# The last gate tile of a decode step cut in halves around two transposes, and six value loads issued from ScalarE

## What is computed

```python
h = rmsnorm(x, norm_attn)
qa, ka, va, qb, kb, vb, qc, gate_logits = split(h @ w_in)      # gate_logits: 3 x 1024 per token
# decode: 8 sequences, caches of 128 (a), 2048 read at strides 1, 4, 16 (b), 256 (c) rows
oa = gathered_attention(qa, [cache_swa_k; ka], [cache_swa_v; va], idx_a, sink)
ob = dilated_sample(qb, [cache_dil_k; kb], [cache_dil_v; vb], 2048)
oc = memory_attention(qc, cache_mem_k, cache_mem_v)
g = sigmoid(gate_logits).reshape(B, L, 3, 1024)
merged = g[:, :, 0] * (oa @ w_br_a) + g[:, :, 1] * (ob @ w_br_b) + g[:, :, 2] * (oc @ w_br_c)
x = x + merged @ w_out
x = x + moe_ffn(rmsnorm(x, norm_ffn), ...)                     # top 4 of 32 experts, 12.6 MB of weights each
```

## Time and profile before

| | us |
|---|---|
| median of 3 runs | 1260.06 (1259.14 to 1262.4) |
| the profiled execution, its own time | 1257.38 |
| its span in the profile | 1255.5 |
| PE busy | 1202.7 (96%) |
| DVE busy | 410.5 (33%) |
| ACT busy | 233.7 (19%) |
| mean DMA rate over the span | 400 GB/s |

### The profile page before, as it was taken

One profiled execution on the slowest core, in us unless ns is written; L12 is line 12 of the kernel. 1 busy time (PEld: TensorE's weight loads), 2 busy tenths in 40 slices (PEclk: granted clock), 3 DMA queues, 4 the chain that ended last, 5 costly groups with the idle time before them and its releaser, 6 DMA issues.

```text
span 1255.5 us, 14690 instructions
## 1 busy us (share of the span) xinstructions
PE 1202.7 (96%) x6122; PEld 516.6 (41%) x6122; DVE 410.5 (33%) x917; ACT 233.7 (19%) x459; POOL 74.2 (6%) x79
## 2 busy tenths in 40 slices
PE   9999999999999999999998999899999999899996
PEld 4456678775533333333333333333333333333332
DVE  3275653335531422314132222313131323222233
ACT  2212433230210210111211011111011121101112
POOL 0453000510200000000000000000000000000000
PEclk9999999999999999999999999999999999999998
DMA  9999999999999999999999999999999999999994
GB/s 337 388 312 365 325 352 355 269 346 395 353 409 429 428 434 433 431 434 429 429 433 431 433 432 432 431 430 432 432 432 431 430 431 432 433 433 421 430 425 172
DMA packets 64712, 502.36 MB, mean 400 GB/s; under 512 B 5872, under 2 KB 30064, under 8 KB 48112
## 3 DMA queue, kind: packets, MB, share of 16 engines
q1 hardware_dynamic: 62784, 497.10, 97.1%
q0 software_dynamic: 848, 2.36, 0.6%
q10 hardware_dynamic: 1008, 1.90, 0.4%
HBM read 498.42 MB, written 37.03 MB: 426 GB/s over the span
## 4 chain that ended last, share of the span: by engine, by line
PE 58%; DMA 33%; SPq 5%; DVE 2%; issue 1%; ACT 0%; DVEq 0%; ACTq 0%
PE ps L1902 19%; DMA ring<-in_w_gate_up 19%; PE ps L1945 11%; DMA high<-in_w_gate_up 6%; PE ps L1268 6%; DMA high<-in_w_down 4%; PE ps L1799 3%; DMA low<-in_w_gate_up 3%; PE ps L1354 3%; PE ps L1861 3%; PE ps L1649 2%; SPq L610 2%; PE ps L1662 2%; DMA ring<-in_w_in 2%; PE ps L1818 1%; PE ps L1330 1%
## 5 line engine op out<-in xcount | busy, mean ns | idle before, releaser
L1902 PE MATMUL ps<-ring,high 128*64 128x512 f32 x1216 | 272.3, 595 | 17.8 <-DMA ring<-in_w_gate_up 17.6
L1902 PEld LDWEIGHTS ps<-ring,high 128*64 128x64 f32 x1216 | 85.8, 136 | 181.7 <-issue 155.1
L1945 PE MATMUL ps<-ring,high 128*64 128x512 f32 x608 | 138.2, 596 | 0.7 <-issue 0.7
L1354 PE MATMUL ps<-low,ring 128*128 128x288 f32 x384 | 102.1, 413 | 0.3 <-DMA ring<-in_w_in 0.3
L1150 ACT ACTIVATE high<-ps 128x512 f32<-128x512 f32 x32 | 19.1, 597 | 439.8 <-PE ps L1921 439.8
L1902 PE MATMUL ps<-high 128*64 128x512 f32 x416 | 93.4, 595 | 7.8 <-DMA high<-in_w_gate_up 7.8
L1902 PE MATMUL ps<-low,high 128*64 128x512 f32 x416 | 93.0, 595 | 5.2 <-DMA low<-in_w_gate_up 5.2
L2443 DVE TENSOR_REDUCE low<-ps 128x1 f32<-128x288 f32 x15 | 6.9, 458 | 274.5 <-PE ps L1831 274.5
L1354 PEld LDWEIGHTS ps<-low,ring 128*128 128x128 f32 x384 | 69.7, 190 | 22.5 <-issue 5.3
L1945 PEld LDWEIGHTS ps<-ring,high 128*64 128x64 f32 x608 | 42.6, 136 | 75.4 <-issue 72.2
L2471 DVE TENSOR_TENSOR x_tok<-x_tok,ps 64x512 f32<-64x512 f32 (+2 forms) x48 | 41.3, 860 | 74.7 <-PE ps L1861 72.4
(11 more groups left out here) (381 smaller groups left out, 1198.8 us busy)
## 6 DMA issues: line engine op xcount, KB each, us to landing
ring<-in_w_gate_up SPq DMA_DIRECT2D x28, 4096.0 KB, 38.1
ring<-in_w_down SPq DMA_DIRECT2D x14, 4096.0 KB, 40.6
ring<-in_w_gate_up SPq DMA_DIRECT2D x20, 2048.0 KB, 26.9
high<-in_w_gate_up SPq DMA_DIRECT2D x10, 4096.0 KB, 37.7
low<-in_w_gate_up SPq DMA_DIRECT2D x9, 4096.0 KB, 38.4
ring<-in_w_down SPq DMA_DIRECT2D x10, 2048.0 KB, 19.4
low<-in_w_down SPq DMA_DIRECT2D x5, 4096.0 KB, 38.9
high<-in_w_down SPq DMA_DIRECT2D x5, 4096.0 KB, 39.5
```

The lines of the kernel that those rows point to most:

```text
L1354: ins = pe.matmul(gate_out(m), wblk[AREA[6 + m // 4]][:, k, (m % 4) * P:(m % 4 + 1) * P], hT_v[:, k, :], start=(k == 0), stop=(k == KC - 1))
L1902: ins = pe.matmul(bank(gu0 + u)[64 * h:64 * h + 64, :], xTe[:, k % 4, (k // 4) * 64:(k // 4) * 64 + 64], every_other_four(pair_buf[slot][: ...
L1945: ins = pe.matmul(bank(7 if last else 5)[64 * h:64 * h + 64, :], aT[:, kk % 4, (kk // 4) * 64:(kk // 4) * 64 + 64], pair_buf[slot][:, a:a ...
```

## The change

Three things move, and no arithmetic is added.

1. Tile 23 no longer follows sequence 5. Its first half (k 0 to 3) comes after the products that make the decode result, and its second half (k 4 to 7) after the two transposes.
2. For b = 5, 6 and 7, `cache_swa_v` and `cache_mem_v` are issued by ScalarE and no longer by SP. ScalarE waits for the same `s_pv_done`.
3. `o_tok` moves out of `hT`, which tile 23 still reads, into an area of the ring. ScalarE makes the sigmoids of channels m = 0 to 6 before it copies tile 23, and m = 7 after it.

```diff
-        o_tok = hT[:, 0:256]
+        o_tok = aux[:, 2432:2688]
...
-        GATES_IN_VALUES = (1, 3, 5)
+        GATES_IN_VALUES = (1, 3)
...
+        def load_other_values(eng, b):
+
+            s, sm = vslot[b % NVS], val_in[b % NVS]
+            eng.dma_start(cache_a(s), d["cache_swa_v"][0, b].rearrange("r h n -> r (h n)")).then_inc(sm, 16)
+            eng.dma_start(cache_c(s), d["cache_mem_v"][0, b].rearrange("(r p) h n -> p r (h n)", p=P)).then_inc(sm, 16)
...
-                sp.dma_start(cache_a(s), d["cache_swa_v"][0, b].rearrange("r h n -> r (h n)")).then_inc(sm, 16)
-                sp.dma_start(cache_c(s), d["cache_mem_v"][0, b].rearrange("(r p) h n -> p r (h n)", p=P)).then_inc(sm, 16)
+                if b < NVS:
+                    load_other_values(sp, b)
...
-            for _ in GATES_IN_VALUES:
+            for b in range(NVS, NB_S):
+                act_e.wait_ge(S["s_pv_done"], b - NVS + 1)
+                load_other_values(act_e, b)
+                if b == NVS:
+                    evict_gate()
+            for _ in GATES_IN_VALUES[1:]:
                 evict_gate()
             act_e.wait_ge(S["s_tok_done"], 1)
             act_e.activation(o_tok[:, P:2 * P], bank(5)[:, 0:P], ACT.Copy).then_inc(S["s_tokb_evicted"], 1)
-            act_e.wait_ge(S["gate_evicted"], 24)
+            act_e.wait_ge(S["gate_evicted"], 23)
...
             for m in range(8):
+                if m == 7:
+                    evict_gate()
+                    act_e.wait_ge(S["gate_evicted"], 24)
...
             ins.then_inc(S["s_tok_done"], 1)
+            gate = gate_open()
+            gate_products(gate, range(KC // 2))
             pe.wait_ge(S["s_tokb_evicted"], 1)
             pe.transpose(bank(6)[:, P:2 * P], o_tok[:, P:2 * P], ident)
             pe.wait_ge(S["s_toka_evicted"], 1)
             pe.transpose(bank(6)[:, 0:P], o_tok[:, 0:P], ident).then_inc(S["s_ot_done"], 1)
+            gate_products(gate, range(KC // 2, KC))
...
+            pe.wait_ge(S["gate_evicted"], 24)
             for n in range(2):
                 pe.wait_ge(S[f"wo{n}_in"], 16)
```

More of the change, by code:

```diff
@@ L1607, in _ @@
                     gate_tile()
-            assert gate_n[0] == 24
             pe.wait_ge(S["osel_ready"], 1)
@@ L1637, in _ @@
             pe.transpose(bank(6)[:, 0:P], o_tok[:, 0:P], ident).then_inc(S["s_ot_done"], 1)
+            gate_products(gate, range(KC // 2, KC))
+            assert gate_n[0] == 24
             pe.wait_ge(S["s_o_evicted"], 1)
```

## The result

| | before | after |
|---|---|---|
| median, us | 1259.22 (6 runs) | 1264.09 (6 runs, 1263.22 to 1266.42) |
| profiled execution, us | 1257.38 | 1263.76 |
| its span, us | 1255.5 | 1261.9 |
| start of the branches, us | 262.58 | 265.49 |

The ratio of the runs is 1.0042, with a 95% interval of 1.0027 to 1.0056 (it is worked out over the runs, and need not be the quotient of the two medians, here 1.0039). The kernel is slower by 4.9 us, where +7.5 was predicted; the time lies inside the range. By the number alone the rivals A (1263.2) and B (1262.7) fit better than the forecast (1267.6); what decides between them is the profile. The two profiled executions are 6.4 us apart, because that of before lies 1.8 us under its median and that of after 0.3 us.

The account below looks back on a forecast made before the run. From 365 us the stream of expert weights through the DMA engines was taken as the bound, not PE. Late w_out +9.7 less 2.2 from holes gave +7.5 on 1260.06: 1267.6 us, range 1262.4 to 1269.6.

Parts of the forecast that it names:

- Rival A: Decode values: issuing is the limit, values arrive by 251.5, PE does not wait; +3.1 us, 1263.2; chance 0.13.
- Rival B: Stream start: PE's position decides, missing DMA time does not reach the end; 1258.3 or 1262.7; chance 0.12.
- Term 1: End of decode attention: halves of tile 23, 2.08 us each, fill PE's idle 0.89 + 0.16 + 0.52 = 1.57 us.
- Term 2: Sequences 6 and 7: tile 23 had covered late value loads, so PE waits and the branches start 2.6 us later.
- the bound by bytes: Sequence 7's values: moving bytes, not issuing, is the limit, so nothing is gained and they land at 256.3.
- The cost that I put at nothing: Sequence 5: ScalarE's loads for sequences 6 and 7 run beside its loads, making it about 1 us late.
- Term 3: Second branch block: waits for tile 23, DMA engines stand from about 255 to 266, w_out lands 9.7 us later.
- Term 4: Before 365 us: three later holes where DMA engines ran dry close and take up 2.2 us of the lateness.

Follow-up runs that it names:

- tile only: The change with all value loads back on SP, tile 23 still in halves around the transposes; ratio 1.0048 to the kernel before.
- loads only: The change with tile 23 put back behind sequence 5, undivided, and ScalarE's six value loads kept; ratio 1.0029 to the kernel before.
- loads later: As loads only, but ScalarE issues the loads of sequences 6 and 7 only when sequence 4 is done; ratio 0.9995 to the kernel before.
- copies ahead: The change, with SP issuing the two remaining cache copies (4 MB) ahead of the second branch block; ratio 1.0023 to the kernel before.
- PE delayed: The change, with four more dummy products on PE ahead of the first expert, 2.6 us added; ratio 1.0054 to the kernel before.
- kept kernels: The change or tile only, with tile 23's weights copied aside so the second branch block need not wait for it; ratios 1.0042, 1.0042, 1.0040 to before.
- tile only, kept: Tile only (value loads on SP), with tile 23's weights copied aside so the second branch block goes out behind the values; ratio 1.0040 to before.
- kept again: The kernel of kept run a second time, beside the change; ratio 1.0042 to the kernel before.
- kept: The change, with VectorE copying tile 23's weights aside so the second branch block need not wait for tile 23; w_out waits instead; ratio 1.0042 to before.

## Why the prediction was right

**Term 1** held where the halves stand: the 0.16 and 0.52 us around the transposes are gone, and the halves take 2.21 and 2.11 us, where 2.08 was expected. The 0.89 us ahead of sequence 7 became 0.68, with the waits of term 2 ahead of it.

**Term 2** (the tile covered the values; +2.6 us at the branches) held, with +2.7 to +2.9. Where PE waits did not come out: 2 to 3 us ahead of sequence 6 and about 2 ahead of 7 were expected, and PE waits 3.70 ahead of 5, 1.12 ahead of 6 and 0.68 ahead of 7. The last landing was expected at 255.6; the last values came at 256.2, as in the bound by bytes (256.3). The Trainium skill, page "DMA: Bandwidth & Descriptors", section "Rules for kernel authors", was right here that issuing from several engines gives no bandwidth: change and tile only start sequence 7 at 256.24 and 256.52.

The cost that I put at nothing was the reading furthest off: sequence 5 waits 3.70 us, not about 1. In this kernel it cost nothing more, as I said, since sequence 7 waits in any case; in loads only it is the cause of 1.0029, which loads later shows. The Trainium skill, page "DMA: Bandwidth & Descriptors", section "Queues, rings and completion order", has packets taken from the queues in turn. The trace agrees only in part. ScalarE's 64 KB, issued at 233.61, landed after 10.7 us, against 2.8 for 128 KB that met no queue; its queue's packets first moved near 240 us, and from then on shared the engines with SP's loads of sequence 5.

**Term 3** (+9.7 us by the time `w_out` lands) held: 283.9 was read where 282.7 was predicted, and the lag at 284 us is 10.2. That the missing DMA time is a cause was tested by copies ahead, which fed the DMA engines in the gap and changed neither tile nor block: its lag less delay is -0.3 where the change's is 3.1, and its median 1261.84, where tile only, run beside it, has 1263.93.

**Term 4** (-2.2 us, taken up by later holes) is the term that was mis-sized: the holes took up 4.4. I had read them as share, 1.64 + 0.32 + 0.24 us, in three short windows. Read as bytes they are deeper, as the stretch from 328 to 344 ran at 321 GB/s with a share of 0.88, and from 344 to 365 at 400 with 0.99: with a backlog these became 404 and 427, which is 3.1 + 1.3 us. Why the rate before was only 400 at a share of 0.99 the rows do not show. With this, the sum is 10.2 - 4.4 = 5.8, which is the lag read. The profiled executions are 6.4 us apart, 0.6 more, which stays open; from there to the 4.9 between the medians it is the two profiled executions' distance from their medians. So of the 2.6 us between forecast and measurement term 4 is -2.2; term 3 is +0.5, what stays open +0.6, and the medians against the profiled executions -1.5. That the time lies in the range is in part luck: the forecast by itself went from +5.0 to +9, and the range takes in +4.9 only because it also reaches down over rival A, which did not happen. The sum of PE's waits for weights was expected to grow by about 5 us and grew by 2.9.

**Rival A** (values early) is out: no landing moved. **Rival B** (PE's position sets the end) is not what happens in the change, by PE delayed and by copies ahead. But it is right on what comes next. Of the lag of 5.8 us, 2.7 are PE's lateness, and in the kept kernels these stay when the block is early, since the DMA engines stand for the late tile from 262 to 266 and for the late PE at 332 to 340. By the traces the two causes are there at once: the late block is worth 2.6 to 3.1 us more than PE's delay, where terms 2 to 4 implied 9.7 - 2.2 - 2.6 = 4.9.

How the loss divides between the two stays open. The 2.6 to 3.1 us come from the profiled executions, and the timing of copies ahead agrees (2.1 us). The ratios of the kept kernels (1.0042, 1.0042, 1.0040) do not show them: by these alone PE's late start would be the whole cost. The medians are 3.6, 5.6 and 4.4 us over before, against 4.9 and 4.8 for the change. The profiles of tile only, kept and of kept again have the granted clock down and branches at 267.8 and 268.3, and if most timed runs were like these, PE's larger delay would stand in for what the early block saves. That is argued and not shown, as a timed run has no profile; and the profiled run of tile only, kept, with its branches at 267.8, is the fastest of its nine.

## What to carry to other kernels

Before a piece of PE work is moved out of a stretch, ask what it covers there (here 4 us of value loads) and which transfer waits for its last read (here a 2 MB block, and all behind it on the queue). In a kernel bound by a stream of bytes, keep the account of a change as bytes behind, window by window against the kernel before; a hole is as deep as its missing bytes, not as its missing share. Work from a second queue shares the engines with the first, so issue it when its data is next, not when its buffer comes free.

## What the runs showed of the hardware

The granted clock after a wait of PE was not the same from one execution to the next. After 3.70 us of waiting the change's first profile kept 1.00 throughout (2.4 GHz). The same kernel again, after a wait of 3.30 us:

```profile
250.00:254.00 4.00, 2.31 (x22) 0.97 (x22) 0.00 (x0) 0.00 (x0) 3.23 (x4) 0.56 1.11 349
254.00:258.00 4.00, 4.00 (x44) 1.95 (x43) 0.69 (x1) 0.00 (x0) 0.86 (x2) 0.59 0.36 118
```

A mean of 0.56 to 0.59 is mostly the lower level, 1.2 GHz. Of the eleven profiles with a wait of PE of over 2 us between 246 and 266 us, eight show the granted clock at 0.50 to 0.79 in the windows behind it (waits of 2.17 to 4.14 us), and three keep 1.00 (the longest waits 2.62, 2.94 and 3.70). The length of the wait alone does not tell which. The end of the kernel shows the same: three profiles have a wait of 2.61 us for weights near 1210 us. After it 16 products take 5.35 us in copies ahead and in loads later, and 3.65 in kept, with the granted clock at 0.59, 0.79 and 1.00 from 1212 to 1216.
